# Six zeroed products before the first matmul, another PSUM bank for MoBA's last head, and its last gate in five pieces

## Chip, core and metric

One Trainium2 chip, one core in use. Time is device time in microseconds (us); the kernel is launched once and the median of several launches is given. The engines: TensorE (PE; its weight loads are shown apart as PEld), VectorE (DVE), ScalarE (ACT), GpSimd (POOL), SyncE (SP, which only issues DMAs here). Everything is fp32. TensorE writes to the eight banks of PSUM (128 partitions x 512 fp32 each). TensorE runs at one of two clock levels, 1.2 and 2.4 GHz.

## The reference, cut to what matters

Two transformer blocks in a row over x (256 tokens x 1024). The change touches the first one alone:

```python
h = rmsnorm(x, norm1_w[l])
proj = h @ w_in[l]                      # 1024 x 6656
rq, rk, rv, rg, mq, mk, mv, ga, gb = jnp.split(proj, split_points, axis=-1)
...
ret = jax.nn.silu(rg) * retention(rq, rk, rv)          # 4 heads
a = ret @ w_ret_out[l]
b = moba_attention(mq, mk, mv) @ w_moba_out[l]         # 8 heads of 64
mix = jax.nn.sigmoid(ga) * a + jax.nn.sigmoid(gb) * b
x = x + mix @ w_o[l]
...                                     # swiglu
```

With 256 tokens MoBA has one block, so it is causal softmax attention over all keys. The second block (forgetting attention, latent attention, four swiglus, norms, gates) is not changed.

## The kernel before

**Products of weights.** Every weight goes through TensorE as "units" of 1 MB (128 partitions x 2048 fp32). SyncE loads unit u into `w_raw[u % 3]`. ScalarE makes its upper part `w_hi` (rounded fp32r), VectorE, or GpSimd for the stages in `POOL_STAGES`, the remainder `w_lo = w_raw - w_hi`. Activations are split in the same way (`xTh`, `xTl`), and one product is three matmuls: `mm3` (L572 to L574: xTh·w_hi, xTl·w_hi, xTh·w_lo). A unit of 4 x 128 rows and 512 columns for both token tiles (t = 0, 1, of 128 tokens each) is 24 matmuls.

**`Chunk`** is 512 output columns of one stage in two PSUM banks, one for each token tile. `run(w, tiles=, part=)` issues the products of its unit w, of some tiles, and of the first or second half of the unit's rows. `take(bank, label)` lets TensorE wait until the former content of a bank has been read; `need` waits for a marked instruction of another engine. Both are waits in TensorE's own stream: what stands behind waits too.

**The start.** SyncE issues parts of the transposed x (`xt`) and half units in turn. ScalarE (`keep_xt`, `half_unit`, L1496) and VectorE (L2104, L2118) split them; both work in the order in which they are written. TensorE's first instructions are `entry()` (L927): four groups, for the two halves of units 0 and 1; each group is 8 matmuls with w_hi and 4 with w_lo. After it comes the chunk `rk0` (L619, L626, L634), then `rv0`, `rv1` and so on.

**MoBA** is `attention("moba", ...)`, a pipeline over heads written out by hand. In step s TensorE issues the scores of head s (L883, banks 4 and 5 in turn), the work in `lead` where there is any, the transposes of the weights of head s-1 (`turn`, L568, bank 6), the output of head s-2 (`weigh`, L895 and L896, bank `out_bank`), and then the work in `fill[s]`. The fill is the projections ga and gb in whole units, and the transposes of the retention result (`to_xT("ret", ...)`): `ret` columns 0 to 511 into banks 0 and 1, the others into banks 2 and 3. ScalarE's loop does, in step s, its own `fill[s-1]`, `exps(s)`, `turned(s-1)`, `keep_o(s-2)`. VectorE's does `soft(s)`, `weights(s)`, `rest_o(s-2)`, and then its `fill[s-1]`:

```python
fill[5] = [lambda: xT_evac("ret", (0,), slot0=8)]          # VectorE, step 6, L2252
fill[6] = [lambda: xT_evac("ret", (1,), slot0=8, b0=2)]    # VectorE, step 7
```

Bank 0 and bank 1, which the chunk `gb1` takes next, are free once VectorE's `xT_evac` (L1876) of step 6 has read them. `out_bank` gives bank 7 for every head of MoBA, so `weigh(h)` waits until ScalarE (`keep_o`, L1310) and VectorE (`rest_o`, L2081) have read head h-1 from it. After MoBA come `ret_out0`, `ret_out1` and `moba_out0` on TensorE; the next one to take bank 4 is `to_xT("mix", ...)` behind them.

Of the kernel before, what the change touches and what calls it, by code (L numbers as in the profile page):

```python
# [30 lines left out]
P = 128  # L31
T = 2
S = T * P
# [10 lines left out]
MOBA_H, MOBA_DH = 8, 64  # L44
# [135 lines left out]
def build(nc, dram, marks):  # L180
# [32 lines left out]
    with ExitStack() as ctx:  # L213
        def sb(name, cols, dt=F32):
            return ctx.enter_context(nc.sbuf_tensor(name, [P, cols], dt))
# [3 lines left out]
        def sem(name):  # L219
            sems[name] = ctx.enter_context(nc.semaphore(name))  # L220
            return sems[name]
# [15 lines left out]
        tanh = sb("tanh", T * CH)[:, :].rearrange("p (t n) -> p t n", t=T)  # L237
        gb = sb("gb", 2 * D)[:, :].rearrange("p (a n) -> p a n", a=2)
# [59 lines left out]
        ro = c1b.tiles(T, D)  # L298
# [28 lines left out]
        bank = [low[:, b] for b in range(4)]  # L327
# [20 lines left out]
        p_loaded, aux_loaded, eps_set = sem("p_loaded"), sem("aux_loaded"), sem("eps_set")  # L348
        half_hi, half_lo = sem("half_hi"), sem("half_lo")
        zeros_set, rope_q_loaded = sem("zeros_set"), sem("rope_q_loaded")  # L350
        gates_placed = sem("gates_placed")

        tanh_done = sem("tanh_done")
        hid_part, hid_done = sem("hid_part"), sem("hid_done")
# [7 lines left out]
        def mark(name, *label):  # L362

            counts[name] += 1
            if label:
                assert label not in found, label
                found[label] = (name, counts[name])
            return 1

        def note(label, name, value):  # L370
            assert label not in found, label
            found[label] = (name, value)

        def need(eng, *label):

            if not marks:
                return
            name, value = marks[label]
            if seen.get((eng, name), 0) < value:
                seen[(eng, name)] = value  # L380
                ENG[eng].wait_ge(sems[name], value)
# [97 lines left out]
        @block.gpsimd  # L479
        def _(pool):  # L480
            ENG["pool"] = pool
            pool.memset(eps[:, 0:1], LN_EPS).then_inc(eps_set, 1)
            pool.memset(eps[:, 1:2], RMS_EPS).then_inc(eps_set, 1)
            pool.memset(mask[:, 0:P], 0.0).then_inc(zeros_set, 1)
            pool.wait_ge(zeros_set, 1)
            pool.memset(mkz[64:P, 0], 0.0).then_inc(zeros_set, 1)
            pool.wait_ge(zeros_set, 2)
            pool.memset(mkz[0:64, 1], 0.0).then_inc(zeros_set, 1)
            for u, unit in enumerate(units):
                if u == unit_at["ffn1"][0] + 2:  # L490
                    need("pool", "ffn_out", 0, 1)
                    pool.wait_ge(w_lo_done[(u - 1) % RING], (u - 1) // RING + 1)
                    pool.wait_ge(zeros_set, 3)
                    pool.memset(fkz[64:P, 0], 0.0).then_inc(zeros_set, 1)
                    pool.wait_ge(zeros_set, 4)
                    pool.memset(fkz[0:64, 1], 0.0).then_inc(zeros_set, 1)
                    pool.wait_ge(zeros_set, 5)
                    for n, (rows, value) in enumerate(((fkz[64:66, 0], 1.0), (fkz[0:2, 1], 1.0), (fqz[64:P, 0], -1.0),
                                                       (fqz[0:64, 1], -1.0))):
                        pool.memset(rows, value * FOX_DH ** 0.5).then_inc(zeros_set, 1)  # L500
                        pool.wait_ge(zeros_set, 6 + n)
                if u in pool_units:
                    cols, s = unit[1] * unit[2] or UNIT, slots[u]
                    pool.wait_ge(w_hi_done, u + 1)
                    pool.tensor_tensor(w_lo[s][:, 0:cols], w_raw[u % RING][:, 0:cols], w_hi[s][:, 0:cols].bitcast(F32),  # L505
                                       ALU.subtract).then_inc(w_lo_done[u % RING], 1)
# [5 lines left out]
        def site_ready(site, t, q):  # L512

            return {"ret": ("gated", q, t), "mix": ("ev", f"moba_out{q}", t),
                    "raw": ("ffn_out", 0, t)}.get(site, ("norm", site, t, q))
# [6 lines left out]

        def out_bank(name, h):

            return 7 if name == "moba" or h % 2 == 0 else 3

# [2 lines left out]
        def turn_bank(site, t, q, b):  # L531

            return TURN_BANK[site][2 * t + q] if site in TURN_BANK else b
# [20 lines left out]
        def _(pe):  # L554
# [3 lines left out]
            def take(b, label):  # L558

                if freed[b]:  # L560
                    need("pe", *freed[b])
                freed[b] = label

            def transposes(b, free, label, pairs):

                take(b, free)
                for c, src in pairs:
                    mm = pe.matmul(bank[b][:, c:c + P], src, ident, is_transpose=True, start=True, stop=True)  # L568
                mm.then_inc(pe_done, mark("pe_done", *label))
# [106 lines left out]
            def unit_steps(stage, banks, **kw):  # L676

                c = Chunk(stage, banks, **kw)
                return [(lambda w=w: c.run(w)) for w in range(len(c.us))]

            def to_xT(site, src, qs_=(0, 1), b0=0, between=None, tiles=range(T)):

                for t in tiles:
                    if t and between:
                        between()
                    for q in qs_:
                        need("pe", *site_ready(site, t, q))
                        transposes(turn_bank(site, t, q, b0 + t * len(qs_) + q - qs_[0]), ("xT", site, t, q), ("T", site, t, q),
                                   [(j * P, src[:, t, (4 * q + j) * P:(4 * q + j + 1) * P]) for j in range(4)])

            def need_xT(site, qs_=(0, 1)):
                for t in range(T):
                    for q in qs_:
                        need("pe", "xT", site, t, q)
# [217 lines left out]
            def tok(t):  # L912
                return slice(t * P, (t + 1) * P)
# [10 lines left out]
            def entry():  # L924

                def product(t, k, a, w, start=False, stop=False):
                    return pe.matmul(bank[t], a[:, k, tok(t)], w[:, k % 4], start=start, stop=stop)  # L927

                for t in range(T):
                    take(t, ("ev", "rq0", t))  # L930
                for u in range(2):
                    wh, wl = (m[slots[u]][:, :].rearrange("p (k n) -> p k n", k=4) for m in (w_hi, w_lo))
                    for half in range(2):
                        ks = range(4 * u + 2 * half, 4 * u + 2 * half + 2)
                        end = u == 1 and half == 1
                        hi, lo = ((w_hi_done, w_lo_done[u]) if half else (half_hi, half_lo))
                        for ts in ((0,), (1,)) if end else ((0, 1),):
                            pe.wait_ge(hi, 1 if half and not u else u + 1)
                            for t in ts:
                                for k in ks:  # L940
                                    need("pe", "xTh", 0, k)
                                    product(t, k, xTh, wh, start=k == 0)
                            for t in ts:
                                for k in ks:
                                    need("pe", "xT", 0, k)
                                    product(t, k, xTl, wh)
                            pe.wait_ge(lo, 1 if half else u + 1)
                            for t in ts:
                                for k in ks:
                                    mm = product(t, k, xTh, wl, stop=end and k == ks[-1])  # L950
                            if end and ts[0] == 0:
                                mm.then_inc(pe_done, mark("pe_done", "full", "rq0", 0))
                    mm.then_inc(w_used, 1)
                note(("full", "rq0", 1), "w_used", 2)

            entry()
            pe.wait_ge(ident_loaded, 16)
            rk = Chunk("rk0", (2, 3), ready="entry")
# [32 lines left out]
            rg1[0]()  # L991
            turn_qk("mnorm", mqk)
            rg1[1]()
            ga0, ga1, gb1 = (unit_steps(f"{n}{c}", ((2, 3), (0, 1))[c]) for n, c in (("ga", 0), ("ga", 1), ("gb", 1)))
            gb0 = Chunk("gb0", (2, 3))
            ga0[0]()
            for i in range(2):
                for t in range(T):
# [5 lines left out]
                      {0: [ga0[1]], 1: [ga1[0]], 2: [ga1[1]], 3: [lambda: gb0.run(0)],  # L1004
                       4: [lambda: gb0.run(1, tiles=(0,)), lambda: to_xT("ret", ro, (0,))],
                       5: [lambda: gb0.run(1, tiles=(1,))],
                       6: [lambda: to_xT("ret", ro, (1,), b0=2)], 7: [gb1[0]]}, {8: [gb1[1]]})
            need_xT("ret")
            chunk("ret_out0", (2, 3), slot0=8)
            chunk("ret_out1", (0, 1), slot0=8)  # L1010
# [38 lines left out]
            for l in range(2):  # L1049
# [55 lines left out]
                if l == 0:  # L1105
# [4 lines left out]
                    _, wh, _, both = gate_weights(u)  # L1110
                    for k in range(KD):
                        need("pe", "xTh", 2, 1, k // 4)
                        pe.matmul(bank[4][0:32 + FOX_H, 0:S], both[:, k, 0:32 + FOX_H], xTh[:, k], start=k == 0,
                                  stop=k == KD - 1)
# [1394 lines left out]
```

## Time and profile before

| | |
|---|---|
| median of 3 runs | 1503.65 us (1503.32 to 1503.71) |
| profiled execution, its own time | 1502.79 us |
| its span, first to last instruction | 1500.7 us |
| TensorE busy | 1480.8 us, 99% of the span |
| VectorE, ScalarE, GpSimd busy | 62%, 53%, 13% |
| mean granted TensorE clock | 0.998 of full speed |
| DMA | 274.73 MB, mean 183 GB/s |

In a timeline each row is: start, duration, engine, line and operation, out<-in, count of merged instructions, and in brackets the idle time before it with what ended it. A matmul's row is longer than its spacing, since matmuls overlap; the spacing of starts is the time it costs. An fp32 matmul (not fp32r) shows as two records.

### The profile page before, as it was taken

How to read it: one execution, taken by the hardware profiler on the slowest of the kernel's cores; microseconds unless marked ns; L12 is line 12 of the kernel's file. 1: busy time of each engine (PE TensorE's matmuls, PEld its weight loads, DVE VectorE, ACT ScalarE, POOL GpSimd, SP SyncE). 2: the span in 40 equal slices, each digit the busy share in tenths (PEclk: the TensorE clock that was granted, in tenths of full speed). 3: DMA queues.
4: the chain of work that ended last, by engine and by line, in shares of the span. 5: the costliest groups of instructions: out<-in, count | busy, mean ns of one | idle time of the engine just before them, and what ended most of it. 6: DMA issues, size and time to landing. Idle time of an engine off the chain costs nothing.

```text
span 1500.7 us, 21356 instructions
## 1 busy us (share of the span) xinstructions
PE 1480.8 (99%) x8040; PEld 1282.4 (85%) x8040; DVE 934.2 (62%) x1219; ACT 799.8 (53%) x987; POOL 189.6 (13%) x56
## 2 busy tenths in 40 slices
PE   8999999999999999999999999999999999999997
PEld 6888788888888888898888888888888998888886
DVE  7575565666656565535776668776666465766667
ACT  6546545444444444667554456654446664544456
POOL 0015211000040000372100001000005451100010
PEclk9999999999999999999999999999999999999999
DMA  9545356665546555552565557565555335565562
GB/s 344 196 141 178 120 181 200 214 194 196 191 159 211 189 183 179 181 169 85 196 210 185 193 196 226 178 214 184 190 195 164 123 113 196 188 203 188 183 215 74
DMA packets 187545, 274.73 MB, mean 183 GB/s; under 512 B 10048, under 2 KB 137184, under 8 KB 187488
## 3 DMA queue, kind: packets, MB, share of 16 engines
q1 hardware_dynamic: 183568, 262.77, 52.9%
q10 hardware_dynamic: 3920, 11.18, 2.4%
q8 instruction: 39, 0.64, 0.2%
q14 instruction: 18, 0.15, 0.0%
HBM read 272.83 MB, written 1.05 MB: 183 GB/s over the span
## 4 chain that ended last, share of the span: by engine, by line
PE 91%; DVE 5%; ACT 3%; issue 1%; DMA 0%; DVEq 0%; SPq 0%; ACTq 0%
PE bank L710 23%; PE bank L717 12%; PE acc L573 7%; PE acc L572 7%; PE acc L574 7%; PE bank L572 6%; PE bank L574 6%; PE bank L573 6%; PE bank L756 3%; PE acc L883 2%; PE acc L568 2%; PE bank L619 2%; PE bank L626 2%; PE bank L634 2%; DVE w_lo L1836 1%; PE bank L927 1%
## 5 line engine op out<-in xcount | busy, mean ns | idle before, releaser
L1836 DVE TENSOR_TENSOR w_lo<-w_raw,w_hi 128x2048 fp32r<-128x2048 f32 (+1 forms) x208 | 473.0, 2278 | 158.2 <-ACT w_hi L1386 121.4
L710 PE MATMUL bank<-xT,w_hi 128*128 128x512 f32 x1520 | 361.2, 390 | 0.0
L505 POOL TENSOR_TENSOR w_lo<-w_raw,w_hi 128x2048 fp32r<-128x2048 f32 (+1 forms) x41 | 176.4, 4308 | 1267.9 <-ACT w_hi L1302 1267.9
L710 PEld LDWEIGHTS bank<-xT,w_hi 128*128 128x128 f32 x1520 | 282.5, 188 | 56.7
L1386 ACT ACTIVATE w_hi<-w_raw 128x2048 fp32r<-128x2048 f32 x145 | 276.5, 1907 | 0.0
L1302 ACT ACTIVATE w_hi<-w_raw 128x2048 fp32r<-128x2048 f32 (+4 forms) x105 | 189.6, 1818 | 30.2 <-DMA w_raw<-in_w_in 9.4
L717 PEld LDWEIGHTS bank<-xT,w_lo 128*128 128x128 f32 x1520 | 189.3, 192 | 3.9
L717 PE MATMUL bank<-xT,w_lo 128*128 128x256 f32 x1520 | 191.4, 283 | 0.0
L573 PE MATMUL acc<-w_lo,sTh 128*128 128x512 f32 x400 | 155.7, 389 | 0.0
L572 PE MATMUL acc<-w_hi,sTh 128*128 128x512 f32 x400 | 155.7, 389 | 0.0
L574 PE MATMUL acc<-w_hi,sTl 128*128 128x512 f32 x400 | 155.6, 389 | 0.0
L572 PE MATMUL bank<-w_hi,xT 128*128 128x512 f32 (+1 forms) x304 | 119.5, 393 | 0.0
L574 PE MATMUL bank<-w_hi,xT 128*128 128x512 f32 (+1 forms) x304 | 117.0, 385 | 0.0
L573 PE MATMUL bank<-w_lo,xT 128*128 128x512 f32 (+1 forms) x304 | 116.7, 384 | 0.0
L1397 ACT ACTIVATE squares<-bank 128x512 f32<-128x512 f32 x50 | 29.9, 597 | 139.6 <-PE bank L717 139.6
L1408 ACT ACTIVATE sTh<-hid 128x512 fp32r<-128x512 f32 x45 | 28.5, 632 | 134.9 <-PE acc L574 134.9
L574 PEld LDWEIGHTS acc<-w_hi,sTl 128*128 128x128 f32 x400 | 75.1, 188 | 15.6
L572 PEld LDWEIGHTS acc<-w_hi,sTh 128*128 128x128 f32 x400 | 75.1, 188 | 15.5
L573 PEld LDWEIGHTS acc<-w_lo,sTh 128*128 128x128 f32 x400 | 75.1, 188 | 15.4
L1397 ACT ACTIVATE tanh<-bank 128x512 f32<-128x512 f32 x45 | 26.8, 597 | 106.3 <-PE bank L710 106.3
L572 PE MATMUL bank<-xT,w_hi 128*128 128x256 f32 x271 | 78.5, 290 | 0.3 <-ACT arena L1310 0.3
L574 PE MATMUL bank<-xT,w_lo 128*128 128x256 f32 x271 | 76.7, 283 | 0.0
(225 smaller groups left out, 2061.1 us busy)
## 6 DMA issues: line engine op xcount, KB each, us to landing
w_raw<-in_ffn_w_in SPq DMA_DIRECT2D x176, 512.0 KB, 4.4
w_raw<-in_ffn_w_out SPq DMA_DIRECT2D x88, 512.0 KB, 4.2
w_raw<-in_w_in SPq DMA_DIRECT2D x52, 512.0 KB, 4.8
w_raw<-in_fox_w_in SPq DMA_DIRECT2D x24, 512.0 KB, 4.6
w_raw<-in_w_ffn_gate SPq DMA_DIRECT2D x22, 512.0 KB, 4.7
w_raw<-in_w_ffn_up SPq DMA_DIRECT2D x22, 512.0 KB, 4.5
w_raw<-in_w_ffn_down SPq DMA_DIRECT2D x22, 512.0 KB, 4.2
w_raw<-in_ple_w_gate SPq DMA_DIRECT2D x16, 512.0 KB, 4.5
```

The costliest lines, as they stand in the source:

```text
L505: pool.tensor_tensor(w_lo[s][:, 0:cols], w_raw[u % RING][:, 0:cols], w_hi[s][:, 0:cols].bitcast(F32), ALU.subtract).then_inc(w_lo_done[u % ...
L568: mm = pe.matmul(bank[b][:, c:c + P], src, ident, is_transpose=True, start=True, stop=True)
L572: pe.matmul(out, ah, bh, start=first, stop=False, skip_group_check=biased)
L573: pe.matmul(out, ah, bl, start=False, stop=False, skip_group_check=biased)
L574: return pe.matmul(out, al, bh, start=False, stop=last, skip_group_check=biased)
L710: mm = pe.matmul(bank[b + m], wh[:, k, m], both, start=k == 0 and not narrow_first, stop=k == KD - 1 and narrow_first, skip_group_check=na ...
L717: mm = pe.matmul(bank[b + m][:, S:], wl[:, k, m], xTh[:, k], start=k == 0 and narrow_first, stop=k == KD - 1 and not narrow_first, skip_gr ...
L756: mm = pe.matmul(out, (xTl if part == 1 else xTh)[:, k, tok], both[:, k], start=part == 0 and k == 0, stop=last and k == KD - 1)
L1302: nc.scalar.activation(hi, raw, ACT.Copy).then_inc(w_hi_done, 1)
L1386: nc.scalar.activation(w_hi[slots[u]][:, :], w_raw[u % RING][:, :], ACT.Copy).then_inc(w_hi_done, 1)
L1397: nc.scalar.activation(dst.rearrange("p (m n) -> p m n", m=2), low[:, b:b + 2, S:], ACT.Copy)\
L1836: nc.vector.tensor_tensor(w_lo[s][:, 0:cols], w_raw[u % RING][:, 0:cols], w_hi[s][:, 0:cols].bitcast(F32), ALU.subtract).then_inc(w_lo_don ...
```

## The change

Three edits. (1) GpSimd's first instruction zeroes 256 columns of `tanh`, and TensorE issues six fp32 products 128x128 · 128x256 of it into bank 7 before `entry()`; their result is read by nobody. (2) `out_bank` gives bank 4 for head 7 of MoBA. (3) The chunk `gb1` is issued in five pieces, by token tile, from step 6 on, in place of two whole units in steps 7 and 8.

```diff
+        gates_placed, idle_set = sem("gates_placed"), sem("idle_set")
...
+            pool.memset(tanh[:, 0, 0:S], 0.0).then_inc(idle_set, 1)
             pool.memset(eps[:, 0:1], LN_EPS).then_inc(eps_set, 1)
...
-            return 7 if name == "moba" or h % 2 == 0 else 3
+            if name == "moba":
+                return 4 if h == MOBA_H - 1 else 7
+            return 7 if h % 2 == 0 else 3
...
+            pe.wait_ge(idle_set, 1)
+            for _ in range(6):
+                pe.matmul(bank[7][:, 0:S], tanh[:, 0, 0:P], tanh[:, 0, 0:S], start=True, stop=True)
             entry()
...
-            ga0, ga1, gb1 = (unit_steps(f"{n}{c}", ((2, 3), (0, 1))[c]) for n, c in (("ga", 0), ("ga", 1), ("gb", 1)))
+            ga0, ga1 = (unit_steps(f"ga{c}", ((2, 3), (0, 1))[c]) for c in range(2))
+            gb1 = Chunk("gb1", (0, 1))
...
-                       6: [lambda: to_xT("ret", ro, (1,), b0=2)], 7: [gb1[0]]}, {8: [gb1[1]]})
+                       6: [lambda: to_xT("ret", ro, (1,), b0=2), lambda: gb1.run(0, tiles=(0,))],
+                       7: [lambda: gb1.run(0, tiles=(1,)), lambda: gb1.run(1, tiles=(0,), part=0)]},
+                      {8: [lambda: gb1.run(1, tiles=(0,), part=1), lambda: gb1.run(1, tiles=(1,))]})
```

The last dictionary is `lead`: its work stands before `turn` in step 8.

## Rows read from the trace of the kernel before

**Rows 1.** Waits of TensorE, whole span: releaser, us in total, times, longest.
```profile
PE bank L927 <- ACT w_hi L1496: 6.7, 1, 6.7
PE acc L568 <- DVE arena L2073: 1.4, 4, 0.5
PE acc L895 <- DVE sTl L2081: 0.9, 1, 0.9
```
**Rows 2.** Timeline of the first 16 us, all engines.
```profile
0.82 0.21 POOL L484 MEMSET mask<- 128x128 f32 x1
4.26 0.91 ACT L1310 ACTIVATE xT<-arena 128x256 fp32r<-128x256 f32 x2 [1.56 <-DMA arena<-in_xt]
6.67 1.23 DVE L2118 TENSOR_TENSOR w_lo<-w_raw,w_hi 128x1024 fp32r<-128x1024 f32 x1 [0.99 <-ACT w_hi L1496]
6.70 3.57 PE L927 MATMUL bank<-w_hi,xT 128*128 128x512 f32 x8 [6.70 <-ACT w_hi L1496]
7.78 1.06 ACT L1496 ACTIVATE w_hi<-w_raw 128x1024 fp32r<-128x1024 f32 x1 [0.34 <-DMA w_raw<-in_w_in]
10.10 1.09 PE L927 MATMUL bank<-w_lo,xT 128*128 128x512 f32 x4
10.41 1.71 ACT L1310 ACTIVATE xT<-arena 128x256 fp32r<-128x256 f32 x4 [1.57 <-DMA arena<-in_xt]
12.03 1.99 ACT L1496 ACTIVATE w_hi<-w_raw 128x1024 fp32r<-128x1024 f32 x2
13.11 2.56 DVE L2118 TENSOR_TENSOR w_lo<-w_raw,w_hi 128x1024 fp32r<-128x1024 f32 x2 [0.47 <-ACT w_hi L1496]
13.76 1.98 PE L927 MATMUL bank<-w_hi,xT 128*128 128x512 f32 x8
```
**Rows 3.** Timeline of TensorE, 6 to 21 us: where `rk0` begins.
```profile
19.20 1.07 PE L619 MATMUL bank<-w_hi,xT 128*128 128x512 f32 x4
```
**Rows 4.** Chain of waits up to 220 us: start, duration, what.
```profile
30.24 0.23 PE bank L572
64.68 0.43 PE acc L974 x2
```
**Rows 5.** Timeline of VectorE, 19 to 76 us.
```profile
26.88 4.49 DVE L1836 TENSOR_TENSOR w_lo<-w_raw,w_hi 128x2048 fp32r<-128x2048 f32 x2
```
**Rows 6.** Timeline of TensorE, 128 to 184 us.
```profile
156.13 0.82 PE L883 MATMUL acc<-arena 128*128 128x128 f32 x4
157.69 0.47 PE L572 MATMUL bank<-w_hi,xT 128*128 128x512 f32 x1
163.21 0.82 PE L883 MATMUL acc<-arena 128*128 128x128 f32 x4
164.57 0.55 PE L568 MATMUL acc<-ident,arena 128*128 128x128 f32 x3 [0.53 <-DVE arena L2073]
165.56 0.48 PE L572 MATMUL bank<-w_hi,xT 128*128 128x512 f32 x1
176.55 0.49 PE L568 MATMUL acc<-ident,arena 128*128 128x128 f32 x3
178.61 0.70 PE L895 MATMUL acc<-arena 128*128 128x256 f32 x2 [0.92 <-DVE sTl L2081]
179.28 0.48 PE L572 MATMUL bank<-w_hi,xT 128*128 128x512 f32 x1
```
**Rows 7.** Timelines of ScalarE, VectorE and GpSimd, 148 to 184 us.
```profile
161.40 1.26 ACT L1310 ACTIVATE arena<-bank,neg_mean 128x512 f32<-128x512 f32 x2
177.07 0.49 ACT L1310 ACTIVATE arena<-acc 128x384 f32<-128x384 f32 x1 [6.75 <-PE acc L568]
164.76 1.27 DVE L1876 TENSOR_TENSOR xT<-bank,xT 128x512 fp32r<-128x512 f32 x2
170.35 2.29 DVE L1836 TENSOR_TENSOR w_lo<-w_raw,w_hi 128x2048 fp32r<-128x2048 f32 x1
161.46 4.55 POOL L505 TENSOR_TENSOR w_lo<-w_raw,w_hi 128x2048 fp32r<-128x2048 f32 x1 [7.77 <-ACT w_hi L1302]
```

More of the change, by code:

```diff
@@ L350, in build @@
         zeros_set, rope_q_loaded = sem("zeros_set"), sem("rope_q_loaded")
-        gates_placed = sem("gates_placed")
+        gates_placed, idle_set = sem("gates_placed"), sem("idle_set")
         tanh_done = sem("tanh_done")
```

## Prediction

> **What bounds the kernel now.** I read the page's busy times first: TensorE is busy for 1480.8 of 1500.7 us, so only time that TensorE stands still, or works slowly, is to be had. The view of TensorE's waits gives where it stands still [rows 1]: 6.7 us before its very first matmul, 0.9 us once at L895 before MoBA's last output, and 1.4 us in four waits for attention weights (L568). The change aims at the first two. Then I read the timelines around both places. At the start the reader is to see that eight matmuls take from 6.70 to 10.10, and that from 10.10 on the pace is another [rows 2]. At 163 to 180 us the reader is to see who else is working in the banks that the moved gate wants [rows 6, 7].
>
> **Part 1: six products in front.** What TensorE did before: it was idle until 6.70. The eight matmuls from there take 10.10 - 6.70 = 3.40 us, 0.425 each; the 40 from 10.10 to the start of `rk0` at 19.20 take 9.10 us, 0.2275 each [rows 2, 3]. That is the 1.2 GHz level after idleness and the 2.4 GHz level after some work, though the granted-clock column shows 1.00 in both stretches; the spacing is what I go by. If all eight ran at the upper level, 8 x (0.425 - 0.2275) = 1.58 us would go.
>
> What the six products cost: one fp32 product with 256 moving columns is two records and takes 0.43 us at the upper level [rows 4]; at the lower one, by 0.425 / 0.2275 = 1.87 or at most by 2, 0.80 to 0.86. Six take 4.8 to 5.2 us (an estimate). They start when GpSimd's memset of 256 columns is done; 128 columns took 0.21 [rows 2], so about 0.42 at most, in front of instructions that began at 0.8: about 1.2. They end at 6.0 to 6.4, before ScalarE's first half of `w_hi` is there at 6.70. Behind TensorE's new wait stands its whole stream, which would wait for `w_hi` until 6.70 anyway. On GpSimd the two `eps`, the mask and the `mkz` memsets come 0.3 to 0.4 us later. ScalarE waits for `eps` to load its table, and its first work after that starts only at 4.26, on a DMA [rows 2]. That cover is over a microsecond; without it the 0.4 us would be the price. Bank 7 and `tanh` have no other user for tens of microseconds.
>
> What is late next: with 24 matmuls of unit 0 at 0.2275, TensorE is at unit 1 at 6.70 + 5.46 = 12.16. On the way the inputs are there: the first `w_lo` at 6.67 + 1.23 = 7.90 against 8.52, the second `w_hi` at 7.78 + 1.06 = 8.84 against 9.43. But the first half of unit 1 is split by ScalarE from 12.03 on, 1.99 us for two halves, behind the parts of x that wait for a DMA at 10.41; VectorE gets that half at 13.11 [rows 2]. TensorE gets it then too, instead of 13.76. From there 24 matmuls: 13.11 + 5.46 = 18.57 in place of 19.20. **Gain 0.63 us of the 1.58**; the other 0.95 becomes a wait in `entry`. That wait is also slack: the six products may end 0.9 us late, or five matmuls of the entry may still be slow (5 x 0.1975 = 0.99), and the gain is the same. The ends are 0 and 0.63.
>
> Does it last? The next supply that is near is the first unit of `rv0`: `w_lo` for two units from 26.88 in 4.49 us, the first at about 29.13 [rows 5], wanted at 30.24 [rows 4], now at 29.61. 0.5 us of margin, so it holds. Afterwards the DMA runs at half load and the chains on VectorE and ScalarE start from TensorE's own results, so they move with it.
>
> **A rule on the clock.** The row shows slow matmuls after 6.7 us of idleness and fast ones after 3.4 us of work [rows 2]. The Trainium skill ("TensorE: Matmul & The Clock Gate", Part 1) says that the throttled state is the default and activity releases it; the same page, in "HAM oscillation", says that idle gaps between bursts bring it back, and that speaks against this edit, because a gap of 0.3 to 0.7 us is left before 6.70. A gap that long did no harm at 178.61: after 0.92 us idle, the next weigh took 179.28 - 178.61 = 0.67 [rows 6]. By the first part of the rule the sum is as above; by the second, the whole gain of part 1 goes.
>
> **Part 2: head 7 into bank 4.** `weigh(7)` waited 0.92 us for VectorE to read bank 7 [rows 6]. Bank 4 was last read for head 6's weights, long before, and is next taken by the "mix" transposes behind three chunks. So the bank is free; what is late next is head 7's own transposed weights: `turn(7)` at 176.55, ScalarE's copy from 177.07 for 0.49 [rows 6, 7], so 1.01 us after the turn's start. With 0.05 for the handover and 0.67 for the weigh itself, `ret_out0` starts 1.73 us after `turn(7)`; before it was 179.28 - 176.55 = 2.73. **Gain 1.00 us.**
>
> **Part 3: the gate in five pieces.** The same 48 matmuls; 12 of them go from behind `weigh(5)` to before `scores(7)`. It is meant to cover the wait of `turn(6)` for its weights, 0.53 us [rows 6], and it does. But `gb1` tile 0 takes bank 0, and bank 0 holds the transposed `ret`, which VectorE reads in its step 6, behind head 6's weights: two instructions from 164.76 in 1.27 us, so the first is done at 164.76 + 0.68 = 165.44 (L1876's median in that stretch is 0.68) [rows 7]. In the old order TensorE came to bank 0 at 165.56, just too late to notice. In the new one it comes at 163.21, where it now begins `scores(7)` [rows 6], and stands until 165.48: **2.27 us of new wait**. Everything in the in-order stream waits with it, `scores(7)` and `turn(6)` among it, so the chain of head 7 starts 5 us later too; it is covered by the 36 matmuls (8.2 us) in front of `turn(7)`.
>
> VectorE isn't sooner at bank 0 for that: it stands behind the softmax of head 6, and that behind ScalarE's gate copies at 161.40 to 162.66 [rows 7], all of which belong to work that TensorE issued before the moved piece.
>
> The sum of parts 2 and 3: from 165.48, 48 matmuls (165.56 to 176.55 is 10.99 us), scores + turn + weigh undisturbed (156.13 to 157.69, 1.56 us), and the 1.73 of part 2: 165.48 + 10.99 + 1.56 + 1.73 = 179.76, against 179.28 before. A restart after a wait that is contained in 10.99 (0.1) may be counted twice, so +0.4: **cost 0.4 us, where 1.0 was gained by the bank and 1.4 lost by the pieces**. Without the wait it would be 163.21 + 10.99 + 1.56 + 1.73 = 177.49, a gain of 1.8. These are the two ends.
>
> What runs later on the others is hidden: the `w_lo` of `ret_out0`'s first unit, at 170.35 for 2.29 [rows 7], comes behind head 7's softmax, some 3 to 5 us later, at 175 to 178, and is wanted at 179.7. GpSimd's remainder of the gate's second unit is done at 161.46 + 4.55 = 166.01, and wanted after 170 [rows 7].
>
> **Sum.** -0.63 + 0.40 = -0.2 us. The profiled execution took 1502.79 us (span 1500.7 and 2.1 around it), 0.86 less than the median; what lies around the span stays, so 1502.6 for it and 1503.65 - 0.2 = 1503.4 for the median.
>
> **The rivals.**
> - The gate pays in full: bank 0 is free when the piece comes, and the 1.8 us stand. For it: the wait would be for one short VectorE instruction. Against it: that instruction's place in VectorE's order, and 164.76 in the row. -0.63 - 1.8 = -2.4: 1501.2.
> - Slower: the clock isn't up when `entry` begins, because the six products don't raise it or the gap before 6.70 takes it back. Place: the eight matmuls from 6.70. Part 1 is then worth 0, and part 3's wait is left alone: +0.4, 1504.05. It decides from the sixth or seventh slow matmul on: unit 1 would have to start after 13.34 for less than 0.4 gained, that is 1.18 us late, six matmuls at 0.1975. For it: only 5 us of thin work (two records per product, always the same operands) lies in front. Against it: in the row 3.4 us of work were enough.
> - The change at the start doesn't shorten anything, since the entry is bound by its loads: true for 0.95 of the 1.58 us by my own sum. If the DMA of x or unit 1 lands 0.6 us later, all of it is; the result is again 1504.0. For it: the DMA is at full load there. Against it: TensorE started unit 1 at 13.76, 0.65 after its input.
>
> **Chances.** The forecast 0.62; the gate in full 0.15; the clock lost 0.11; the loads 0.05; other things (a later wait that swallows or adds some, up to 1 us and more) 0.07. The time is the forecast's, 1503.4. Its own range is 1502.9 to 1503.9. With the slower cases and a run-to-run spread of 0.4 us the upper end is 1504.5; downward I go part of the way to the gate in full, 1501.9. About 0.2% (3.0 us) is what can be told from no change here; all named cases lie within it: same 0.93, faster 0.04 (the gate in full and something with it), slower 0.03.
>
> **What would show it.** In the profile after: six products (12 records) on TensorE from about 1.2 to 6.4; L927's first eight matmuls in 1.8 us instead of 3.4; a new wait of about 0.9 us inside L927, for ScalarE; `rk0` at about 18.6. Near 163 us (0.6 earlier by then) a wait of about 2.2 us of L572 for VectorE's L1876, no wait at L568 for head 6, and at L895 no wait for VectorE's L2081. Wrong would be: L572 without such a wait (then the gate's rival), `rk0` at 19.2 (then one of the other two), or a difference that arises after 200 us, where I expect nothing.

## The result: 2.1 us slower, and the profile after

The changed kernel takes 1505.54 us (median of 22 runs) against 1503.41 us of the kernel before (22 runs): the medians are 2.1 us apart. The ratio is 1.0012 (95% interval 1.0007 to 1.0018); it is one of means, 1.8 us apart, without the two slow runs of the kernel before, 1634.93 and 4369.25 us. Forecast were 1503.4 us and a range that ended at 1504.5. The prediction was wrong. The runs fall into two groups, 16 at 1505.4 to 1505.9 and 6 at 1503.9 to 1504.3, with nothing between. The profiled execution took 1505.56 us with a span of 1503.3, 2.6 more than before.

First TensorE's waits, as in [rows 1], four lines of the view:

```profile
PE acc L961 <- POOL tanh L482: 1.1, 1, 1.1
PE bank L930 <- ACT w_hi L1505: 0.9, 2, 0.5
PE bank L575 <- DVE xT L1885: 2.1, 1, 2.1
PE bank L575 <- DVE w_lo L1845: 1.0, 1, 1.0
```

Besides those at the start, two lines are new, both at L575 (the old L572). The first was forecast, the second wasn't. The start, timeline of TensorE, answers [rows 2, 3]:

```profile
1.11 5.21 PE L961 MATMUL acc<-tanh 128*128 128x256 f32 x12 [1.11 <-POOL tanh L482]
6.72 2.11 PE L930 MATMUL bank<-w_hi,xT 128*128 128x512 f32 x8 [0.40 <-ACT w_hi L1505]
8.67 1.07 PE L930 MATMUL bank<-w_lo,xT 128*128 128x512 f32 x4
12.99 2.11 PE L930 MATMUL bank<-w_hi,xT 128*128 128x512 f32 x8 [0.54 <-ACT w_hi L1505]
18.57 1.07 PE L622 MATMUL bank<-w_hi,xT 128*128 128x512 f32 x4
```

As forecast: products from 1.1 to 6.3, the first eight matmuls in 8.67 - 6.72 = 1.95 us, a new wait at unit 1, `rk0` at 18.57. That the last agrees to the hundredth is luck: unit 1 began at 12.99, not at 13.11, because ScalarE came to it 0.13 us sooner in this execution (at 11.90, not 12.03), and its 24 matmuls took 18.57 - 12.99 = 5.58 us, not 5.46. The wait was 0.54 us, not 0.95.

The timeline of TensorE at MoBA's end, 161 to 185 us, answers [rows 6]:

```profile
164.88 0.50 PE L575 MATMUL bank<-w_hi,xT 128*128 128x512 f32 x1 [2.11 <-DVE xT L1885]
165.22 0.40 PE L576 MATMUL bank<-w_lo,xT 128*128 128x512 f32 x1
...
166.41 0.63 PE L575 MATMUL bank<-w_hi,xT 128*128 128x512 f32 x1
166.83 0.63 PE L576 MATMUL bank<-w_lo,xT 128*128 128x512 f32 x1
167.26 0.63 PE L577 MATMUL bank<-w_hi,xT 128*128 128x512 f32 x1
...
168.97 1.20 PE L886 MATMUL acc<-arena 128*128 128x128 f32 x4
170.00 0.49 PE L571 MATMUL acc<-ident,arena 128*128 128x128 f32 x3
...
179.20 0.49 PE L571 MATMUL acc<-ident,arena 128*128 128x128 f32 x3
...
180.94 0.48 PE L575 MATMUL bank<-w_hi,xT 128*128 128x512 f32 x1
...
184.94 0.50 PE L575 MATMUL bank<-w_hi,xT 128*128 128x512 f32 x1 [1.00 <-DVE w_lo L1845]
```

Look at the starts, not at the durations: after the wait they are 0.23 us apart, from 166.41 to 168.97 they are 0.43 apart, from 171.2 on 0.23 again. Head 7's scores take 170.00 - 168.97 = 1.03 us. In the kernel before, those at 156.13 [rows 6] took 0.66, up to this line of the same view:

```profile
156.79 0.49 PE L568 MATMUL acc<-ident,arena 128*128 128x128 f32 x3
```

The table of busy time by stretch says why. Its columns: stretch, its length, busy us and count of PE, PEld, DVE, ACT, POOL, then the granted clock, DMA share, GB/s:

```profile
165.00:166.00 1.00, 1.00 (x5) 0.82 (x6) 0.42 (x1) 0.00 (x0) 0.38 (x1) 1.00 0.00 0
166.00:167.00 1.00, 1.00 (x5) 0.79 (x4) 0.00 (x0) 0.00 (x0) 0.00 (x0) 0.66 0.30 66
167.00:168.00 1.00, 1.00 (x4) 0.81 (x3) 0.00 (x0) 0.00 (x0) 0.00 (x0) 0.50 0.90 322
168.00:169.00 1.00, 1.00 (x4) 0.71 (x4) 0.00 (x0) 0.00 (x0) 0.00 (x0) 0.50 1.05 406
169.00:170.00 1.00, 1.00 (x5) 0.87 (x4) 0.00 (x0) 0.00 (x0) 0.00 (x0) 0.63 0.66 256
170.00:171.00 1.00, 1.00 (x9) 0.95 (x8) 0.64 (x4) 0.12 (x1) 0.00 (x0) 1.00 0.00 0
```

The granted clock falls to 0.50 (1.2 GHz) about 1.5 us after TensorE went back to work at 164.88, and stays there for about 3.4 us. PE counts as busy all the while, and the page's clock row, tenths of 38 us slices, shows nothing.

The last line to read is 184.94: `ret_out0`'s second unit waits for its `w_lo`. VectorE, 175 to 187 us:

```profile
182.60 2.29 DVE L1845 TENSOR_TENSOR w_lo<-w_raw,w_hi 128x2048 fp32r<-128x2048 f32 x1 [1.39 <-ACT w_hi L1311]
```

It ends at 184.89. In the kernel before, the same unit started at 182.29; TensorE, 170 to 195 us, and VectorE, 148 to 184 us:

```profile
181.89 0.39 PE L574 MATMUL bank<-w_hi,xT 128*128 128x512 f32 x1
182.29 0.50 PE L572 MATMUL bank<-w_hi,xT 128*128 128x512 f32 x1
179.94 2.29 DVE L1836 TENSOR_TENSOR w_lo<-w_raw,w_hi 128x2048 fp32r<-128x2048 f32 x1 [1.39 <-ACT w_hi L1302]
```

184.94 - 182.29 = 2.65 us is nearly the whole difference of the two executions (2.6 by the spans, 2.77 by their own times).

### The profile page after: what moved, and what is told of

Read it like the earlier page. It is cut to its first block, busy times and chain, and to the rows that moved or that the text cites. A ratio compares the mean times of both kernels' runs of the same rounds, so it can differ in the third digit from the quotient of the medians.

```text
span 1503.3 us, 21380 instructions
## 1 busy us (share of the span) xinstructions
PE 1486.4 (99%) x8052; PEld 1286.2 (86%) x8052; DVE 934.3 (62%) x1219; ACT 800.0 (53%) x987; POOL 189.8 (13%) x57
## 4 chain that ended last, share of the span: by engine, by line
PE 89%; DVE 6%; ACT 3%; issue 1%; DMA 0%; SPq 0%; DVEq 0%; ACTq 0%
PE bank L713 23%; PE bank L720 12%; PE acc L575 6%; PE acc L576 6%; PE acc L577 6%; PE bank L575 6%; PE bank L577 6%; PE bank L576 6%; PE bank L759 3%; PE acc L886 2%; PE acc L571 2%; PE bank L622 2%; PE bank L629 2%; PE bank L637 2%; DVE tanh L1929 1%; DVE w_lo L1845 1%
## 5 line engine op out<-in xcount | busy, mean ns | idle before, releaser
L575 PE MATMUL acc<-w_hi,sTh 128*128 128x512 f32 x400 | 155.7, 389 | 0.0
L575 PE MATMUL bank<-w_hi,xT 128*128 128x512 f32 (+1 forms) x304 | 120.1, 395 | 3.1 <-DVE xT L1885 2.1
L575 PEld LDWEIGHTS acc<-w_hi,sTh 128*128 128x128 f32 x400 | 75.1, 188 | 15.5
L575 PE MATMUL bank<-xT,w_hi 128*128 128x256 f32 x271 | 78.5, 290 | 0.3 <-ACT arena L1319 0.3
```

What stands on the lines that cost most here:

```text
L575: pe.matmul(out, ah, bh, start=first, stop=False, skip_group_check=biased)
```

## Experiments

All times are medians; a ratio is to the kernel before in the same series, with its 95% interval. Those intervals are 0.0009 to each side, as wide as many of the effects, so I read small effects from traces and from how the runs cluster. The kernel before spread over 1.3 to 1.9 us in each of the three series (1502.7 to 1504.6 in all), which turned out to be part of the answer.

The theory after the result: (a) the wait for bank 0 lets the clock fall, 1.6 us; (b) bank 4 buys nothing, because `ret_out0`'s second unit hangs on another chain. Rivals: the slow stretch belongs to other engines' traffic; the bank's gain is real and lost elsewhere.

**The six products alone** (edit 1 only).

> Only the six products in front of the entry, the gate and bank 7 as before. Both theories on the loss expect the same here: rk0 begins at 18.57 instead of 19.20, with 0.9 us of waits inside L927-s groups, and the 0.63 us stay to the end: 1503.4 - 0.6 = 1502.8 us, ratio 0.9996. Rival: the gain at the start is swallowed by a later wait (for w_lo at rv0 or the head chains at 130 us): then rk0 is early and the time is 1503.4.

Measured 1502.40 us, 10 of 11 runs between 1502.29 and 1502.86, ratio 0.9994 (0.9985 to 1.0003). `rk0` at 18.68. The interval includes 1, but nine of the 11 runs lie below the lowest of 33 of the kernel before (1502.73). So they help, by 1.1 us of medians, more than the 0.6 expected. Why is seen below: [rows 2] were a lucky start.

**The bank alone** (edit 2 only).

> Only head 7-s output into bank 4. Theory: ret_out0-s second unit is wanted 12 matmuls after its first, its w_lo comes 5.69 us after turn(7) begins, by a chain through keep_o(6), ScalarE-s w_hi and VectorE-s pass that the bank doesn-t touch; weigh(7) and ret_out0 begin 1.0 us earlier, a new wait of about 1 us stands before the second unit, and the time stays 1503.4 (ratio 1.0000). Rival, the sum of the prediction: the 1.0 us is gained, 1502.4 (0.9993).

Measured 1503.98 us, ratio 1.0002 (0.9993 to 1.0011). Its TensorE waits:

```profile
PE bank L574 <- DVE w_lo L1838: 1.0, 1, 1.0
PE acc L570 <- DVE arena L2075: 0.5, 1, 0.5
```

L895's wait of 0.9 is gone and one of 1.0 stands at the second unit. `turn(7)` began at 177.37, the unit at 183.11: 5.74 us, and 182.29 - 176.55 = 5.74 before. The bank alone moves nothing; this execution took 0.76 us more than the one of [rows 3], and that is `rk0`, 19.98 instead of 19.20. (b) holds.

**The pieces alone** (edit 3 only).

> Only the five pieces. A wait of 2.1 to 2.3 us for bank 0 near 163.2; turn(7) 1.5 us later by that wait alone (1504.9 us). Theory with the clock: after the wait the spacing of matmuls is 0.43 us for some 3.5 us, which costs another 1.6, 1506.5 us in most executions and 1504.9 in the others. Rival without it (the slow stretch belonged to the six products): 1504.9 in all, spacing 0.23.

Measured 1505.17 us, ratio 1.0011 (1.0002 to 1.0020). The profiled execution took 1505.98, granted clock 0.69 in 165 to 170 us, wait 2.11. The fall of the clock needs no six products in front. The other part of the expectation missed: "most executions" at 1506.5 weren't there. The runs (1504.8 to 1506.0) show no clean groups, and their median is 1.6 us above that of before, what the wait alone would give. The profiled one is the second highest. In how many of the 11 the clock fell isn't shown; without the six products, the chance of the start lies over them.

**The whole change once more.** No edit; it was run to see another execution's trace.

> The change once more, another execution. Its 22 runs fell into two groups, 16 at 1505.4 to 1505.9 and 6 at 1503.9 to 1504.3. Theory: the wait of 2.1 us for bank 0 is in both; in the upper group the matmuls behind it run slow for 3.5 us, in the lower they don-t. So either 1505.5 with a slow stretch, or 1504.1 without one; a time of one group with the other-s trace would speak against it.

It fell into the lower group of the 22, 1504.0 us. TensorE's timeline and the stretches, as above:

```profile
164.89 0.50 PE L575 MATMUL bank<-w_hi,xT 128*128 128x512 f32 x1 [2.10 <-DVE xT L1885]
...
167.75 0.82 PE L886 MATMUL acc<-arena 128*128 128x128 f32 x4
...
177.57 0.49 PE L571 MATMUL acc<-ident,arena 128*128 128x128 f32 x3
...
183.31 0.50 PE L575 MATMUL bank<-w_hi,xT 128*128 128x512 f32 x1 [1.00 <-DVE w_lo L1845]
```
```profile
166.00:167.00 1.00, 1.00 (x6) 0.83 (x5) 0.00 (x0) 0.00 (x0) 0.00 (x0) 1.00 0.33 98
167.00:168.00 1.00, 1.00 (x8) 0.84 (x7) 0.00 (x0) 0.00 (x0) 0.00 (x0) 1.00 0.91 311
```

Same program, same wait, clock 1.00, and `turn(7)` 179.20 - 177.57 = 1.63 us earlier; the times differ by 1505.56 - 1504.0 = 1.56. This sizes (a) alone. Both waits are there in both executions: they aren't what the groups differ in. The DMA isn't either, since its share in 167 to 168 us is 0.90 and 0.91. Why the clock falls in one execution and not in the other stays open.

**Products in the wait** (on the whole change).

```diff
+            def busy():
+                need("pe", "weights", "moba", 5)
+                for _ in range(4):
+                    pe.matmul(bank[5][:, 0:S], mqT[:, 0, 0:P], mqT[:, 0, 0:S], start=True, stop=True)
...
-                       6: [lambda: to_xT("ret", ro, (1,), b0=2), lambda: gb1.run(0, tiles=(0,))],
+                       6: [lambda: to_xT("ret", ro, (1,), b0=2), busy, lambda: gb1.run(0, tiles=(0,))],
```

> The whole change as it is, with four fp32 products (8 records, 1.7 us) into bank 5 put into the wait for bank 0; nobody reads them. Clock theory: the piece-s first matmul begins at 164.9 as before, but the wait is broken up, the spacing stays 0.23, and turn(7) and all behind it come 1.6 us earlier: 1503.9 (against 1505.5 of the change). Rival (slow spacing comes from the traffic of ScalarE, VectorE and GpSimd at that time, not from TensorE-s idleness): 1505.5.

Measured 1504.03 us, all 11 runs in 1503.8 to 1504.3, ratio 1.0003 (0.9994 to 1.0012). The upper group is gone. More work for TensorE, 1.5 us less time than the 1505.54 of the change; no unchanged copy of it was run in the same series, so this compares two series. Its timeline:

```profile
162.89 1.89 PE L1012 MATMUL acc<-arena 128*128 128x256 f32 x8
165.16 0.50 PE L575 MATMUL bank<-w_hi,xT 128*128 128x512 f32 x1 [0.38 <-DVE xT L1890]
```

GpSimd, VectorE and ScalarE do the same from 160 to 166 us as in the change, all 0.28 us later, and the DMA share in 167 to 169 us is 0.93 and 1.02, as there. The granted clock is 1.00. So the rival is out: it is TensorE's own idleness that lets the clock fall.

**Bank 0 read a step earlier.** VectorE stood idle for 1.3 us just before head 6's softmax, and what this eviction reads had been written over 3 us before. Edit, on the whole change:

```diff
-            fill[5] = [lambda: xT_evac("ret", (0,), slot0=8)]
+            fill[4].append(lambda: xT_evac("ret", (0,), slot0=8))
```

> The whole change, but VectorE reads the transposed ret out of banks 0 and 1 one step earlier (behind head 5-s weights, where it stood idle). No wait at the gate-s first piece, clock at the upper level throughout. turn(7) at about 175.1; by the theory that ret_out0-s second unit comes 5.7 us after it, 1.4 us in all are gained: 1502.0 (0.9991). Rival, the prediction-s sum with bank 4 worth 1.0: 2.4 us gained, 1501.0 (0.9984). Third: if the slow spacing has nothing to do with the wait, it remains and the time is about 1503.7.

Measured 1501.68 us (1501.58 to 1501.92, 11 runs), ratio 0.9988 (0.9979 to 0.9997). `turn(7)` at 175.30, expected 175.1; the unit at 181.04, again 5.74 later; clock 1.00 from 155 to 185 us. One moved VectorE instruction pair turns the change from 2.1 us slower into 1.9 faster. The third theory falls, and so does the prediction's sum with 1.0 for the bank.

**Bank 4 with the unit split earlier** (edit 2 on the kernel before, and):

```diff
-                       7: [lambda: split_to(unit_at["gb1"][0] + RING)], 8: [lambda: keep_gate("gb", 1)]})
+                       7: [lambda: split_to(unit_at["gb1"][0] + RING + 1)], 8: [lambda: keep_gate("gb", 1)]})
...
+            fill[7].append(lambda: split_to(unit_at["gb1"][1] + RING))
```

> Before, with head 7-s output in bank 4 and ret_out0-s second unit split (w_hi, w_lo) in step 8 before head 6-s output is kept, where ScalarE and VectorE stood idle for 5 us. Theory: with the w_lo out of the way the bank-s 1.0 us is gained, and the 0.27 us that stood at that unit before: 1502.1 to 1502.4 (0.9991 to 0.9993). Rival (the bank is worth nothing for another reason): 1503.4.

Measured 1502.12 us, ratio 0.9990 (0.9981 to 0.9999). From `turn(7)` (177.93) to the unit (182.50) it is 4.57 us, no longer 5.74, a gain of 1.17. ScalarE does both `w_hi` in its idle time:

```profile
169.78 3.72 ACT L1304 ACTIVATE w_hi<-w_raw 128x2048 fp32r<-128x2048 f32 x2
178.45 0.49 ACT L1312 ACTIVATE arena<-acc 128x384 f32<-128x384 f32 x1 [4.95 <-PE acc L570]
```

**Everything with both mends.**

> The whole change with both mends: VectorE reads banks 0 and 1 a step earlier, and ret_out0-s second unit is split in step 8. No wait of TensorE over 0.2 us between 163 and 190. Sum: 0.63 at the start, 0.8 by the pieces, 1.0 and 0.27 by the bank: 2.7 us, 1500.7 (0.9982). If the bank is worth nothing: 1502.0.

Measured 1500.38 us (1500.24 to 1500.55, 11 runs), ratio 0.9980 (0.9971 to 0.9989), the fastest of all. No wait of TensorE stands in 155 to 195 us.

**The same without the pieces.**

> The six products, head 7 in bank 4, and ret_out0-s second unit split in step 8, but the gate in whole units as before. Theory: the parts add up, 1502.4 of the products alone less 1.2 for bank and unit: 1501.2 us, with a spread below 0.5 us, since the six products take the start-s chance away. All three with the pieces were at 1500.4, so the pieces would be worth 0.8. Rival (the pieces are worth nothing once the rest is mended): 1500.4.

Measured 1501.12 us (1500.99 to 1501.37, 11 runs), ratio 0.9985 (0.9976 to 0.9994). The pieces are thus worth 0.7 us once bank 0 is free in time. The medians are of two series; the traces say the same, 180.68 - 179.97 = 0.71 us at the second unit.

**Three products instead of six.**

> Three products instead of six in front of the entry, else before. They end at about 3.7 and leave 3 us idle before 6.70. If the work itself is what raises the clock, 2.6 us may be too little, the eight matmuls are slow, and the time is 1503.4 (1.0000), in part of the executions 1502.8. If three do, 1502.8 as with six.

Measured 1503.50 us, ratio 1.0001 (0.9992 to 1.0010): nothing.

```profile
1.12 2.93 PE L959 MATMUL acc<-tanh 128*128 128x256 f32 x6 [1.12 <-POOL tanh L482]
6.84 3.78 PE L928 MATMUL bank<-w_hi,xT 128*128 128x512 f32 x8 [2.80 <-ACT w_hi L1500]
10.42 1.89 PE L928 MATMUL bank<-w_lo,xT 128*128 128x512 f32 x4
12.13 2.04 PE L928 MATMUL bank<-w_hi,xT 128*128 128x512 f32 x8
```

Twelve matmuls run slow here (12.13 - 6.84 = 5.29 us, 0.44 each), not the eight of [rows 2]; executions with no product at all have eight to thirteen (below). It doesn't tell whether three are too few, or the 2.8 us behind them too many.

**All profiled executions in one table.** "Unit" is the start of `ret_out0`'s second unit; the last column is the execution's own time less that start.

| kernel | own time | `rk0` | `turn(7)` | unit | rest |
|---|---|---|---|---|---|
| before | 1502.79 | 19.20 | 176.55 | 182.29 | 1320.50 |
| bank only | 1503.55 | 19.98 | 177.37 | 183.11 | 1320.44 |
| pieces only | 1505.98 | 19.19 | 179.83 | 185.57 | 1320.41 |
| bank, unit earlier | 1502.90 | 20.52 | 177.93 | 182.50 | 1320.40 |
| three products | 1504.08 | 20.36 | 177.78 | 183.52 | 1320.56 |
| six products only | 1502.38 | 18.68 | 176.06 | 181.79 | 1320.59 |
| the change | 1505.56 | 18.57 | 179.20 | 184.94 | 1320.62 |
| the change again | 1504.00 | 18.58 | 177.57 | 183.31 | 1320.69 |
| products in the wait | 1504.23 | 18.85 | 177.84 | 183.59 | 1320.64 |
| bank 0 earlier | 1501.63 | 18.70 | 175.30 | 181.04 | 1320.59 |
| products, bank, unit | 1501.23 | 18.70 | 176.10 | 180.68 | 1320.55 |
| all mended | 1500.43 | 18.77 | 175.40 | 179.97 | 1320.46 |

Four readings. The rest is 1320.4 to 1320.7 in all twelve: everything is decided before 186 us, and nothing is swallowed later. Without the six products `rk0` begins anywhere from 19.19 to 20.52, with them from 18.57 to 18.85: the products remove a chance of 1.3 us, not only the 0.63. From `rk0` to `turn(7)` it is 157.35 to 157.42 us with the gate in whole units; with the pieces it is 160.6 where the clock fell, 159.0 where it didn't, and 156.6 with bank 0 read earlier. Against whole units the pieces thus lose 1.6 us by the wait for bank 0 and another 1.6 by the clock, and gain 0.8 without that wait. And where the second unit isn't split earlier, it starts 5.73 to 5.75 us after `turn(7)`, whichever bank head 7 uses.

## Why the prediction was wrong, step by step

- **Start, gain 0.63 us: right** for the execution that the rows came from (18.57 forecast and measured, to the hundredth by two errors of 0.12 us that cancel), too small for the median. The slow spacing of just eight matmuls was one draw: by their spacing, about eleven were slow in the bank-only execution, about thirteen in the one with the unit split earlier, twelve with three products. The median of the products alone is 1.1 us below that of before. The Trainium skill ("TensorE: Matmul & The Clock Gate", Part 1) warns of it: the number of slow matmuls at the start is "run-variable". The traces agree, with eight to thirteen, and by the `rk0` column.
- **The gain lasts through `rv0` and the head chains: right.** The rest column is constant within 0.3 us.
- **The wait for bank 0: right in place and size.** Forecast from 163.21 to 165.48, less 0.63; measured 2.11 us (forecast 2.27) until 164.88 (forecast 164.85).
- **What that wait costs: this step failed.** The sum priced 2.27 us of idleness at 2.27 us. The clock falls behind it and takes another 1.6. That it fell in 16 of 22 runs is read from the two groups, of which one execution each has a trace; the mean granted clock of the runs, 0.997 to 0.998 in the upper group and 0.998 to 0.999 in the lower, fits it. The prediction had weighed the rule on idle gaps of the Trainium skill ("TensorE: Matmul & The Clock Gate", "HAM oscillation"), but only at the gap in front of `entry`, where 0.40 us did no harm. That section's own case is a wait for data much longer than that. At the longest wait that the change makes, the prediction didn't ask. The wait of 0.92 us [rows 6] that it set against the rule says nothing of one twice as long.
- **Bank 4, gain 1.00 us: this step failed too.** "What is late next" was answered with head 7's transposed weights, for `ret_out0`'s start. The prediction doesn't mention its second unit. `Chunk.run` goes by token tile first, so that unit is wanted after 12 matmuls, 2.7 us, and not after 24. Its `w_lo` comes by a chain that the bank doesn't touch: `turn(7)`, ScalarE's copy, `keep_o(6)` behind `weigh(6)`, then `w_hi`, then VectorE. In the kernel before, this wait was already there at 0.17 us, hidden in a step of the starts from 181.89 to 182.29 (0.40 us instead of 0.23). Measured, the bank gains nothing; with the unit split earlier it and the split gain 1.17 us together.
- **The sum**, for the profiled execution: forecast -0.2; without the 1.0 of the bank +0.8; the clock +1.6; together +2.4, measured +2.65. Most of the other 0.25 lies before `turn(7)`: from the end of the wait to it the prediction has 10.99 + 1.56 = 12.55 us, and the second execution, at the upper clock, took 177.57 - 164.89 = 12.68; the 0.1 that the prediction took off as counted twice wasn't. The change of 0.12% lies within the 0.2% that the prediction called no change, though its interval is clear of 1.
- **Rivals.** The slower one named the right mechanism, a clock that isn't up, in the wrong place; the new wait stands in its 1504.05 at no more than its own length. The gate "in full" needed bank 0 free earlier; given that, the pieces do pay, by 0.7 us.

## What to carry to other kernels

Before work is moved forward as filler, ask of its output buffer, not only of its inputs, whether it is free at that time, and who reads it in which order. A wait of some 2 us on TensorE may cost 1.6 us on top of itself, as here, so price the clock at the longest wait that a change makes, and give each small gain the next consumer of each resource in the order that the code really issues. And compare the starts of matmuls with a chance part (here `rk0`) before a difference of 1 us between two executions is explained.

## What the hardware showed

- After 2.11 us idle TensorE first ran at full pace for 1.5 us; only then did the granted clock go to 0.50, for some 3.4 us (stretches 166 to 170 us). The execution of the pieces alone shows it a second time: 2.11 us idle, work from 165.53, clock 0.93, 0.50, 0.50, 0.50 and 0.86 in the stretches from 166 to 171 us. With the same program and the same wait it stayed at 1.00 in another execution. Products that nobody reads, 1.89 us of the wait, kept it at 1.00 in the profiled execution, and no run of 11 was in the upper group.
- Six fp32 products of zeros, 4.5 to 5.5 us, brought `rk0` to 18.57 to 18.85 in all seven profiled executions that had them, so by the spacing the clock was up by about 7 us (the granted-clock column shows 1.00 at the start even where the matmuls are 0.43 us apart). The idle gaps between these products and `entry` did no harm: the longest, 1.26 us ("products, bank, unit"), was followed by eight matmuls in 8.82 - 6.87 = 1.95 us. Three products, 2.9 us, and 2.8 us idle were followed by twelve slow matmuls in the one execution that was profiled.
- With a regular start the kernel's time is more regular too: three kernels with the six products and no wait of 2 us (1501.68, 1501.12, 1500.38) each spread over 0.3 to 0.4 us in 11 runs, the kernel before over 1.6 and 1.9 in two series of 33. The products alone don't ensure it: nine of their 11 runs lie within 0.24 us, but two are 0.5 and 0.9 us above the median, with no trace.
